# Expert blocks of a diffusion backbone: tokens gathered by row quarters, turned by VectorE, and slot picking for two blocks at a time

## The reference

```python
hid = jax.nn.silu(xb @ w_gate[e]) * (xb @ w_up[e])   # xb: tokens of expert e; w: 1024 x 256
return (hid @ w_down[e]) * wt[:, None]               # 256 x 1024
...
return routed_experts(h, idx, w, w_gate, w_up, w_down) + shared
```

## Time and profile before

| | |
|---|---|
| median of 3 runs | 2167.16 us (2162.87 to 2168.2) |
| profiled execution | 2168.04 us, span 2166.2 us |
| TensorE busy | 1829.5 us (84%), mean granted clock 0.94 |
| VectorE, ScalarE, GpSimd busy | 39%, 25%, 20% |
| up matmuls L1198, down matmuls L1211 | 635.3 us, 306.5 us |
| token transposes L1189, hidden transposes L1217 | 121.9 us, 70.5 us |
| DMA | 578.28 MB, mean 267 GB/s |

### The profile page before, as it was taken

One profiled execution on the slowest core, in us unless ns is written; L12 is line 12 of the kernel. 1 busy time (PEld: TensorE's weight loads), 2 busy tenths in 40 slices (PEclk: granted clock), 3 DMA queues, 4 the chain that ended last, 5 costly groups with the idle time before them and its releaser, 6 DMA issues. The chain is left out here.

```text
span 2166.2 us, 39425 instructions
## 1 busy us (share of the span) xinstructions
PE 1829.5 (84%) x11495; PEld 994.9 (46%) x11496; DVE 846.2 (39%) x2832; ACT 541.0 (25%) x1159; POOL 423.7 (20%) x417
## 2 busy tenths in 40 slices
PE   3999799879999999999995489869689888888883
PEld 2545564445445545445552255545444444444441
DVE  2255563363333333334333525543533232232333
ACT  2141352222222222222221204233222222222221
POOL 0001300012222223223220000230122222222220
PEclk8999799999999999999998789969899999999997
DMA  8325410449999788997966552631599999999984
GB/s 279 119 83 195 170 60 0 175 179 367 377 386 348 284 295 329 359 359 285 392 255 259 192 180 102 251 134 31 209 360 380 411 398 410 399 399 405 359 325 178
DMA packets 170112, 578.28 MB, mean 267 GB/s; under 512 B 29468, under 2 KB 34304, under 8 KB 153160
## 3 DMA queue, kind: packets, MB, share of 16 engines
q1 hardware_dynamic: 134304, 515.49, 61.9%
q0 software_dynamic: 29056, 60.07, 7.6%
q10 hardware_dynamic: 6696, 1.98, 0.4%
HBM read 565.73 MB, written 45.75 MB: 282 GB/s over the span
## 5 line engine op out<-in xcount | busy, mean ns | idle before, releaser
L1198 PE MATMUL bank<-arena 128*64 128x256 f32 x5120 | 635.3, 391 | 126.5 <-DMA arena<-in_exp_w_down 83.6
L1198 PEld LDWEIGHTS bank<-arena 128*64 128x64 f32 x5120 | 349.4, 138 | 291.0 <-DMA arena<-in_exp_w_down 89.0
L666 POOL DMA_INDIRECT yrows<-arena x158 | 160.6, 1016 | 831.7 <-ACT arena L897 814.0
L1211 PE MATMUL bank<-arena 128*64 128x512 f32 x1264 | 306.5, 606 | 1.0 <-issue 1.0
L647 POOL DMA_INDIRECT arena<-hrows,arena x164 | 183.1, 1116 | 142.1 <-DVE arena L1640 89.5
L1670 DVE TENSOR_TENSOR arena<-arena,bank 64x256 f32<-64x256 f32 x160 | 68.0, 425 | 347.2 <-ACT arena L881 347.2
L892 ACT ACTIVATE arena<-bank 128x128 f32<-128x128 f32 x158 | 44.2, 280 | 561.0 <-PE bank L1217 561.0
L897 ACT ACTIVATE arena<-bank 128x512 f32<-128x512 f32 x158 | 94.4, 597 | 210.3 <-PE bank L1211 210.3
L963 PE MATMUL bank<-arena 128*128 128x512 f32 (+3 forms) x384 | 131.8, 505 | 11.7 <-DVE arena L1327 11.7
L1635 DVE COPY arena<-bank 128x3 f32<-128x3 f32 x164 | 26.4, 161 | 289.5 <-PE bank L1182 288.8
L1189 PE MATMUL bank<-arena 128*128 128x128 f32 x648 | 121.9, 311 | 8.2 <-DMA arena<-hrows,arena 8.2
(11 more groups left out here) (297 smaller groups left out, 1845.6 us busy)
## 6 DMA issues: line engine op xcount, KB each, us to landing
arena<-in_exp_w_gate SPq DMA_DIRECT2D x128, 1024.0 KB
arena<-in_exp_w_up SPq DMA_DIRECT2D x128, 1024.0 KB
arena<-in_exp_w_down SPq DMA_DIRECT2D x128, 1024.0 KB
arena<-in_w_ada SPq DMA_DIRECT2D x10, 3072.0 KB
arena<-yrows SPq DMA_DIRECT2D x6, 4096.0 KB, 14.8
arena<-in_w_ada SPq DMA_DIRECT2D x8, 2048.0 KB
arena<-in_w_in SPq DMA_DIRECT2D x8, 2048.0 KB
arena<-in_w_out SPq DMA_DIRECT2D x4, 2048.0 KB
```

Of the source, the lines that this page charges most:

```text
L666: pool.indirect_dma_start(out=yrows, out_offset=bass.IndirectOffsetOnAxis(ap=SIXS[u], axis=0), in_=YSB[u], in_offset=None, bounds_check=2 ...
L1198: ins = pe.matmul(bank[b_par][64 * gu:64 * gu + 64, 0:HID], XGT[b_par][:, c, hh, :], wv[:, gu, hh, c, :], start=(c8 == 0), stop=(c8 == 7))
L1211: ins = pe.matmul(bank[2 + b_par][64 * cg:64 * cg + 64, :], HIDT[b_par][:, c, :], wv[:, c, cg * 512:(cg + 1) * 512], start=(c == 0), stop= ...
```

## The change

Seven things change together.

1. `HP`, a copy of the tokens made by VectorE whose quarters of 256 are stored with the eight interleaved columns ahead (`q d c` to `q c d`); `hrows` now has four rows of 1 KB a token. `HP` lies where the shared output `YS` goes, so ScalarE waits for `pool_hr` before it writes that.
2. `gather` issues two indirect DMAs, one for 32 slots each: partitions 32q to 32q+31 hold quarter q.
3. `turn_tokens` is a VectorE transpose in 32 x 32 squares straight into `XGT`; TensorE's four transposes and ScalarE's `xe` are gone.
4. `up` splits the inner width of 256, not gate and up: slots with inner columns 0 to 127 of both on partitions 0 to 63, with 128 to 255 on 64 to 127. `silu` and `product` work on 128 x 128, and `turn_hidden` is one transpose of 128 x 128. Gate and up weights come in 8 KB pieces, down weights in 4 KB ones.
5. `one_hot`, `meta` and the row numbers are made for two blocks at once. Row numbers are spread over the partitions by two small matmuls with the constants `DUP4` and `DUP2` (`spread`), between `slots` and `indices` on VectorE.
6. VectorE's order in the loop is now: turn the tokens of block b+2, `product` of block b+1, and then `indices` and `slots` (u = 0) or `one_hot` (u = 1).
7. The diagonals `DG` are built by ScalarE behind its loop, and the rank operations are split in two around the first turns.

The core of the diff:

```diff
@@ SyncE
-                    w = at(ring[k], 2, 2, 4, HID)
+                    w = at(ring[k], 2, 8 * HID)
...
-                    sp.dma_start(at(ring[k] + 4096, 2 * DM),
-                                 ed[bass.ds(l * NE + e, 1)].rearrange("a (p c) n -> p (a c n)", c=2)).then_inc(sp_land[k], 16)
+                    sp.dma_start(at(ring[k] + 4096, 2, DM),
+                                 ed[bass.ds(l * NE + e, 1)].rearrange("a (c p) n -> p (a c) n", c=2)).then_inc(sp_land[k], 16)
@@ GpSimd
+                    for h in range(2):
+                        pool.indirect_dma_start(out=XG[k][:, 256 * h:256 * h + 256], out_offset=None, in_=hrows,
+                                                in_offset=bass.IndirectOffsetOnAxis(ap=GIX[:, 2 * k + h:2 * k + h + 1], axis=0),
+                                                bounds_check=4 * (T + 1) - 1, oob_is_err=False).then_inc(pool_g[k], 16)
...
-                        pool.wait_ge(v_ix, i * 2 + (u + 4))
-                        pool.wait_ge(pe_x, i * 2 + (u + 2))
+                        if u == 0:
+                            pool.wait_ge(v_ix, i + 3)
+                            pool.sem_inc(pool_go, 1)
+                        pool.wait_ge(v_xt, i * 2 + (u + 3))
                         pool.sem_inc(pool_go, 1)
-                        gather((u + 1) % 2)
+                        gather(u)
@@ TensorE
+                def spread(val_vx, val_ix):
+                    pe.wait_ge(v_vx, val_vx)
                     if val_ix is not None:
                         pe.wait_ge(v_ix, val_ix)
+                    pe.matmul(bank[4][:, 0:4], DUP4, VX[:, 0:4], start=True, stop=True)
+                    pe.matmul(bank[4][:, 4:6], DUP2, VX[:, 4:6], start=True, stop=True).then_inc(pe_sp, 1)
...
+                    wv = at(ring[k], 2, 8, HID)
+                    for c in chunks:
+                        for nh in range(2):
+                            ins = pe.matmul(bank[b_par][64 * nh:64 * nh + 64, 0:HID].rearrange("p (g n) -> p g n", g=2), XGT[b_par][:, c, :],
+                                            wv[:, :, c, P * nh:P * nh + P], start=(c == 0), stop=(c == 7))
...
+                    pe.transpose(bank[5][:, 0:P], HIDB, IDENT).then_inc(pe_h, 1)
...
-                        meta(1 - u, b + 3, b + 4, b + 3)
+                        if u == 0:
+                            meta(i + 4, i + 3)
+                        else:
+                            spread(i + 4, i + 3)
                         slot_now = None if u == 0 else slot
                         e = expert_of(b + 1)
                         slot = pe.snap(e % 3)
-                        pe.wait_ge(a_xe, b + 2)
+                        pe.wait_ge(v_xt, b + 2)
...
-                        turn_tokens(u, i * 16 + 32)
@@ VectorE
+                def one_hot(b, val, chain):
+
+                    es = [expert_of(b + k) for k in range(2)]
+                    if val is not None:
+                        dve.wait_ge(pe_meta, val)
+                    for k in range(2):
+                        chain(dve.tensor_scalar(RR[:, T0:, k:k + 1], GG[:, T0:, bass.ds(es[k], 1)], BASE[:, 0:1], None, ALU.subtract))
+                        chain(dve.tensor_copy(KVP[:, T0:, 3 * k:3 * k + 3], KV[:, T0:, bass.ds(es[k], 1), :].rearrange("p t a c -> p t (a c)")))
+                    chain(dve.tensor_scalar(BASE, BASE, float(P), None, ALU.add))
...
+                def slots(val, val_sp, chain):
...
+                    for k in range(2):
+                        chain(dve.tensor_copy(M3[64 * k:64 * k + 64, 0:3], bank[7][64 * k:64 * k + 64, 3 * k:3 * k + 3]))
                     chain(dve.tensor_scalar(TK[:, 0:1], M3[:, 0:1], 0.0, BIG_ROW, ALU.is_equal, ALU.mult))
                     chain(dve.scalar_tensor_tensor(out=TK[:, 1:2], in0=M3[:, 0:1], scalar=M3[:, 1:2], in1=TK[:, 0:1], op0=ALU.add, op1=ALU.add))
-                    chain(dve.tensor_scalar(GIX[par], TK[:, 1:2], 2.0, COLS[:, 2:3], ALU.mult, ALU.add))
                     chain(dve.tensor_tensor(TK[:, 2:3], TK[:, 1:2], M3[:, 2:3], ALU.add))
-                    dve.tensor_scalar(six, TK[:, 2:3], 2.0, COLS[:, 2:3], ALU.mult, ALU.add).then_inc(v_ix, 1)
...
+                    chain(dve.tensor_scalar(VX[:, 0:4], COLS[:, 10:14], TK[:, 1:2], None, ALU.mult))
+                    dve.tensor_scalar(VX[:, 4:6], COLS[:, 14:16], TK[:, 2:3], None, ALU.mult).then_inc(v_vx, 1)
+
+                def indices(six, val, chain):
+
+                    dve.wait_ge(pe_sp, val)
+                    chain(dve.tensor_scalar(six, bank[4][:, 4:6], COLS[:, 2:3], None, ALU.add))
+                    dve.tensor_scalar(GIX, bank[4][:, 0:4], COLS[:, 5:6], None, ALU.add).then_inc(v_ix, 1)
+
+                def turn_tokens(k, val):
+                    dve.wait_ge(pool_g[k], val)
+                    dve.transpose(XGT[k].rearrange("p c (h s) -> p h c s", h=2),
+                                  XG[k].rearrange("p (h c d) -> p h c d", h=2, c=8)).then_inc(v_xt, 1)
...
+                one_hot(0, None, link)
+                slots(1, None, link)
+                one_hot(2, 1, link)
+                indices(SIXT[:, 0:2], 1, link)
+                slots(2, 1, link)
+                one_hot(4, 2, link)
...
+                rank_weights(TS[:NTS // 2])
+                for k in range(2):
+                    turn_tokens(k, 32)
+                indices(SIXT[:, 2:4], 2, link)
+                slots(3, 2, link)
+                one_hot(6, 3, link)
+                rank_weights(TS[NTS // 2:])
...
-                        dve.wait_ge(pe_meta, b + 4)
-                        dve.wait_ge(pool_g[1 - u], i * 16 + 16 * (1 + u))
-                        rows(1 - u, b + 3, SIXT[:, bass.ds(b + 3, 1)], chain)
-                        one_hot(u, b + 4, chain)
+                        dve.wait_ge(pe_gu, b + 2)
+                        turn_tokens(u, i * 32 + 64)
                         product(1 - u, b + 2, b + 1)
+                        if u == 0:
+                            dve.wait_ge(pool_g[1], i * 32 + 64)
+                            indices(SIXT[:, bass.ds(i * 2 + 4, 2)], i + 3, chain)
+                            slots(i + 4, i + 3, chain)
+                        else:
+                            one_hot(b + 7, i + 4, chain)
                         dve.wait_ge(pool_s[u], i * 16 + 16)
                         dve.tensor_copy(SIXS[u], SIXT[:, bass.ds(b, 1)]).then_inc(v_six, 1)
```

More of the change, by code:

```diff
@@ L383, in build @@
         v_ix = sem("v_ix")
+        v_vx = sem("v_vx")
+        v_xt = sem("v_xt")
         v_hid = sem("v_hid")
@@ L669, in _ @@
                                                 ).then_inc(pool_s[u], 16)
[L670 to L671 removed]
+                for u in range(2):
+                    pool.wait_ge(pool_g[u], pairs * 32 + 64)
                 for u in range(2):
@@ L1173, in expert_of, with meta @@
                     return pe.value_load(TAB[0:1, bass.ds(b, 1)], min_val=0, max_val=NE - 1)
-                def meta(b_par, b, val_oh, val_ix):
-                    e = expert_of(b)
+                def meta(val_oh, val_vx):
                     pe.wait_ge(v_oh, val_oh)
+                    if val_vx is not None:
+                        pe.wait_ge(v_vx, val_vx)
+                    for t in TS:
+                        ins = pe.matmul(bank[7][:, 0:6], OH[:, t, :], KVP[:, t, :], start=(t == T0), stop=(t == NT - 1))
+                    ins.then_inc(pe_meta, 1)
@@ L1215, in turn_hidden @@
                 def turn_hidden():
-                    for c in range(2):
-                        ins = pe.transpose(bank[5][:, c * SLOTS:(c + 1) * SLOTS], HIDB[64:128, c:HID:2], IDENT[64:128, 64:128])
-                    ins.then_inc(pe_h, 1)
-                meta(0, 0, 1, None)
-                meta(1, 1, 2, 1)
-                for j in range(NTS + 1, 2 * NTS):
-                    shared_down(j)
-                turn_tokens(0, 16)
-                meta(0, 2, 3, 2)
-                turn_tokens(1, 16)
+                    pe.transpose(bank[5][:, 0:P], HIDB, IDENT).then_inc(pe_h, 1)
+                for j in range(3):
+                    meta(j + 1, j if j else None)
+                    spread(j + 1, j if j else None)
+                    if j == 0:
+                        for q in range(NTS + 1, 2 * NTS):
+                            shared_down(q)
                 e = expert_of(0)
-                pe.wait_ge(a_xe, 1)
+                pe.wait_ge(v_xt, 1)
                 for k in range(3):
@@ new lines, in rank_weights @@
+                def rank_weights(tiles):
+                    for t in tiles:
+                        for k in range(TOPK):
+                            link(dve.scalar_tensor_tensor(out=LE, in0=CI[:, t, :], scalar=float(k + 1), in1=SC[:, t, :],
+                                                          op0=ALU.is_equal, op1=ALU.mult, accum_out=WK[:, t, k:k + 1]))
+                one_hot(0, None, link)
+                slots(1, None, link)
+                one_hot(2, 1, link)
+                indices(SIXT[:, 0:2], 1, link)
```

(5 more changed lines are left out.)

148 lines of the change are left out of this document (59 added, 89 removed).

## The result

The changed kernel takes 2603.14 us (median of 4 runs, 2598.93 to 2604.93) where the kernel before took 2165.01 us (median of 4 runs, 2161.18 to 2168.20). The ratio is 1.2022, 95% interval 1.1994 to 1.2049: 20% slower. The forecast was 2335 us with a range of 2215 to 2420, so the direction was right and the time lies 183 us above the range. The profiled execution took 2604.41 us.

A forecast was written before the change was run, and what follows sets the result against it. TensorE was taken to bound layer 0 and the weight stream layer 1. To 2168 us it added 127 for layer 0, 35 for layer 1 and 5 ahead of the loops: 2335 us, range 2215 to 2420.

The forecast's parts named there:

- 0.88 us taken off TensorE: Per block: four token transposes removed (0.68 us) and two hidden transposes made one (0.20 us).
- rival D: TensorE's clock falls to 0.9: 6 us of work grow by 0.65 in 158 blocks, about 2435 us; chance 0.13.
- down to `spread`: First half of a pair: `spread` waits for nine small VectorE operations behind the product, starting at 3.21 us, not 1.87.
- down to `meta`: Second half of a pair: `meta` waits for VectorE's bookkeeping behind the product, starting at 3.86 us, not 1.87.
- slot matmuls to up: TensorE's sequencer work (table read, slot, branch) shows behind the wait, before the up matmuls: 1.24 us.
- exposed before down, a pair: Table read before down, no longer covered by token transposes, shows in every second block: 0 to 0.56 us, taken as 0.20.
- two table reads: VectorE, second half, behind the product's dispatch: first 0.86 us, second between nothing and 0.86, taken as 0.40.
- five small operations ahead of the comparison: VectorE, second half, between the table reads and the one-hot comparison: five at 0.225 us each.
- release from VectorE to TensorE: Signal from VectorE's last bookkeeping operation reaches TensorE 0.27 us later, before `spread` or `meta`.
- B: TensorE's reads and branches overlap and cost little after a wait: 0.62 us a block added, 2226 us; chance 0.18.
- C: Product and bookkeeping finish within down's 1.87 us, so no wait; 0.88 us a block saved, 2103 us; chance 0.08.
- E: Half-size gather packets cost as much as full ones, 91 ns: 23 us more in layer 1, up to 2358; chance 0.05.

The follow-up runs named there:

- e1: Changed kernel with `indices` and `slots` (first half of a pair) and `one_hot` (second half) moved ahead of the product on VectorE: 2161.52 us, ratio to before 0.9884.
- e2: Changed kernel with only `indices` and `slots` moved ahead of the product, `one_hot` staying behind it: 2386.88 us.
- e3: Changed kernel with only `one_hot` moved ahead of the product, `indices` and `slots` staying behind it: 2261.76 us.
- e6: Kernel before the change, with only VectorE's product moved ahead of `rows` and `one_hot`: 2667.95 us.
- e5: Changed kernel with TensorE's expert table read and slot worked out ahead of the waits of `meta` and `spread`: 2369.32 us.
- e12: Changed kernel with all bookkeeping ahead of the product, early table read, and the second block's row indices parked in their own buffer: 2140.18 us, ratio to before 0.9818.

## Why the prediction was right and wrong

**Right: the mechanism and its place.** No slack in `v_oh` and `v_vx`, the bookkeeping behind the product, TensorE waiting before `spread` and `meta` in alternate blocks, the sequencer's chain behind that wait, layer 1 set free from the weight stream. e1, e2, e3 and e6 show it from both sides. Of the 0.88 us taken off TensorE, 0.83 show: from the hidden transpose to down it is 1.25 us instead of 2.08.

**Wrong: the clock.** This is the step that failed. I summed all of TensorE's work at the durations of full clock and set the clock aside as rival D. I argued from stretches of 50 us and took 0.9 over the whole block. The granted clock did fall to a mean of 0.86, close to the 0.9 of D, yet the fall comes where it costs most: up at 0.50, right behind the waits, while the idle time ahead of `meta` counts as full clock in the mean (1.00 from 697.70 to 699.90 us, without a matmul). The six chunks cost 225 us where D had 0.65 x 158, about 100. The evidence was there: the very kernel before runs its 24 up matmuls in 4.50 us after one idle stretch of 2.09 us, with a granted clock of 0.59 from 1853 to 1856 us, where one of 1.19 us left them at 2.81 (894.34 in the earlier trace rows):

```profile
1852.84 4.50 PE L1198 MATMUL bank<-arena 128*64 128x256 f32 x24 [2.09 <-DMA arena<-in_exp_w_down]
```

D got a chance of 0.13 and a price less than half its size. The forecast did not weigh that up matmuls can start at the lower clock behind a long wait, as they do behind the waits of `meta`, with 0.50 granted from 700 to 706 us.

**The other terms.** Without the clock's 140 us in layer 0 and 85 in layer 1 the pitches are 9.06 and 8.94 us, against forecasts of 8.80 and 8.65:

| step, us | forecast | measured |
|---|---|---|
| down to `spread` | 3.21 | 2.82 |
| down to `meta` | 3.86 | 4.42 |
| slot matmuls to up | 1.24 | 1.45 |
| exposed before down, a pair | 0.20 | 0.13 |
| VectorE's transpose, hidden | 0.5 to 2.5 | 0.70 |

The two table reads, taken at 0.86 + 0.40, are 1.58 us from product to `one_hot` (718.31 to 719.89): the second adds 0.72 and is hardly hidden behind the first. The five small operations ahead of the comparison take 1.50 us (719.89 to 721.39) and not 1.13: the two copies among them (L1638) start 0.39 and 0.38 us after the operation before them, where the forecast took 0.225 a step. The release from VectorE to TensorE takes 0.05 us (710.78 to 710.83) to 0.14 (699.86 to 700.00) and not 0.27. In sum: clock 225, layer 0 0.26 x 91 = 24, layer 1 0.29 x 65 = 19, edges 14.5 instead of 5, less the 8 of single blocks: 2335 + 269.5 = 2604.5, the profiled execution.

**The rivals.** B (the sequencer overlaps) is refuted by the 1.45 us after every wait and shown possible by e5, with 0.69. C (faster) asked for bookkeeping under 1.07 us; from the end of the product it takes 1.9 us (708.88 to 710.78) and 3.5 (718.60 to 722.08). Put ahead of the product it is hidden, and then the sign of C comes true, with a fifth (e1, 24 us over 158 blocks) to a third (e12, 42 us) of its 0.88 us a block. E (small packets cost as much as full ones) is refuted: the software queue took 6.4% x 16 x 2602.6 = 2665 us of engine time for the same 60.1 MB, before 7.6% x 16 x 2166.2 = 2634. Its premise fails as well: halving the rows did not double the packets. The trace of before has 14,472 packets of 4096 B in that queue, that of after 14,356, at 171 and 172 ns each; the 91 ns of the prediction is a mean over these and some 14,000 packets of 4 to 20 B that take 9 to 12 ns. The same holds for the weights, whose packets the prediction takes to be ruled by their bytes: in the queue q1 of before a packet of 4096 B took 167 ns and one of 8192 B 337.

## What to carry to other kernels

When a change makes TensorE wait, price two things: the wait, and what its clock does to the work behind it (here 225 of 438 us). Look in the timeline of before for the same instructions right after an idle stretch, and use that row and not a mean clock. Ask of each operation in an engine's program not only how long it takes but behind which wait it stands: here the order of two calls alone was worth 20% (1.2022 of before, and 0.9884 in e1). And what waits for someone else should have its register reads done ahead of the wait: in e5 that was worth 234 us.

## What had not been expected

- In the changed kernel matmuls of 2.74 us take 4.1 to 5.4 us after two idle stretches close together, of 1.0 and 0.9 or of 2.4 and 1.2 us (0.50 granted behind the latter), and 2.74 us after one of 1.0 us (e5).
- Moving a table read of TensorE ahead of a wait was worth 234 us, half of it by the clock.
- On chips where the kernel before took 2182 to 2186 us, completion signals of TensorE come 0.5 to 4 us late while GpSimd issues indirect transfers in a row, in every changed kernel traced there but e2, and the changed kernel takes 2636.6 us there instead of 2603.1; where before took 2164 to 2167 there are none. The cause was not found.
